# Dummy products of TensorE in the pauses for three norms: other operands and other forms

## The chip, the core and the metric

The kernel runs on one core of one Trainium2 chip. The metric is the device time of one execution in microseconds (us), as the median over several runs. A core has a matrix engine (TensorE, rows PE, with its weight loads in rows PEld), VectorE (DVE), ScalarE (ACT), GpSimd (POOL) and DMA queues issued by SyncE (SPq). Each engine runs its own list of instructions in order; they wait for one another through semaphores. TensorE multiplies a stationary operand (at most 128 rows by 128 columns, loaded by LDWEIGHTS) by a moving operand of up to 512 columns and writes to PSUM, which is `bank[:, 0..7, 512]` here. Its clock has two levels here, 1.2 and 2.4 GHz; the profile shows the granted share of the full one as PEclk.

## The reference

Two transformer blocks over 256 tokens of width 2048, all in float32. The first has three attention branches, a gated mix, a projection, and a feed-forward layer with a short convolution. The second has 16 more tokens in front (272), a full-attention layer and a layer of gated linear attention. Between the stages stand norms over each token's row:

```python
def rmsnorm(x, g):
    xf = x.astype(jnp.float32)
    y = xf * lax.rsqrt(jnp.mean(xf * xf, axis=-1, keepdims=True) + EPS)
    return (y * g.astype(jnp.float32)).astype(x.dtype)
...
x = x + rmsnorm(mix @ w_out[l], post_mix_g[l])
h = rmsnorm(x, pre_ffn_g[l])
x = x + rmsnorm(conv_ffn(h, w_up[l], conv_w[l], conv_b[l], w_down[l]), post_ffn_g[l])
...
for i in range(DEPTH_2):
    y = rmsnorm_2(h, pre_norm[i])
    ...
    h = h + rmsnorm_2(y, post_norm[i])
```

A norm of the whole row must be known before the next projection can start, so three times in the kernel the projection engine has nothing to multiply while the other engines make the norm.

## The kernel before

Weights (some 390 MB) stream from HBM in units of 128 x 1024 floats through `raw`. ACT rounds each unit to `whi` (line 602), DVE makes the rest `wlo = raw - whi` (line 1214), and TensorE forms each product in three passes of type float32r: whi by ahi, whi by alo, wlo by ahi (`PASSES`). `features` (line 1935) has the weights stationary and 256 or 272 tokens moving; `rows_of_unit` (line 2032) has the tokens stationary and 512 weight columns moving. The program text is the order: each engine's block is written out stage by stage, and no scheduler or planner stands behind it.

The stages on TensorE are, in order: projections of block one, gates, the branches' outputs (`oabc`), `wout`, **pause 1** (b = 1), `up`, `down`, **pause 2** (b = 2), the projections of the attention layer (`aqk`, `av`, `ag`), `aout`, **pause 3** (b = 3), and the stages of gated linear attention (`gqk`, `lr`, `gv`, `gg`, `gout`).

In a pause ACT squares and sums the last rows (line 693), DVE applies the gain, scales and adds to the residual (lines 1304, 1330), ACT squares the new rows (line 713), and DVE writes the normed rows `xn` (line 1393). For b = 1 the residual rows `xtok` themselves go on (line 1337). TensorE then transposes the rows by products with the identity `ident` (`turn_rows`, line 1975), ACT and DVE make `ahi` and `alo` of the result (lines 726 and 1400), and the next stage's first product waits for those (`made` in `features`).

At the head of a pause TensorE runs `keep_busy(b, n)` (line 2050): n products of two constant float32 tiles, `ones` and `ident`, 128 x 128 by 128 x 128, written to a part of PSUM that nobody reads. n is 12 in pause 1 and 36 in pauses 2 and 3. No engine waits for them; behind them on TensorE's own list stand the transposes. A float32 product stands in the trace as two records, a float32r product as one.

Of the kernel before, what the change touches and what calls it, by code (L numbers as in the profile page):

```python
# [17 lines left out]
F32 = mybir.dt.float32  # L18
# [5 lines left out]
P = 128  # L24
D = 2048
KD = D // P
TB = 256
TM = 16
T2 = TB + TM
# [98 lines left out]
def two_blocks_kernel(nc, A, out):  # L128

    ctx = ExitStack()  # L130
    with ctx:
        place_at = [(nc.sbuf_base + 31) // 32 * 32]

        def sb(name, shape, dt=F32, at_=None):

            size = int(np.prod(shape[1:])) * 4
            off = place_at[0] if at_ is None else at_
            t = nc.alloc_sbuf_tensor_at(name, shape, dt, offset=off)
            if at_ is None:
                place_at[0] = off + (size + 31) // 32 * 32  # L140
            return t
# [16 lines left out]
        ahi = sb("ahi", [P, KD * AS], F32R)  # L158
        alo = sb("alo", [P, KD * AS], F32R)
        par = sb("par", [P, N_PAR])  # L160
        ident = sb("ident", [P, P])
        ones = sb("ones", [P, P])
# [14 lines left out]
        def region(*parts, base=None):  # L177

            off, made = R2 if base is None else base, []
            for name, shape, dt in parts:  # L180
                made.append(sb(name, shape, dt, at_=off))
                off += (int(np.prod(shape[1:])) * 4 + 31) // 32 * 32
            assert off <= LIMIT, (parts[0][0], off, LIMIT)
            return made

        def ha(t, k, c0, n):

            return t[:, k * AS + c0:k * AS + c0 + n]
# [36 lines left out]
        ghi, glo, pr = region(("ghi", [P, FT, TB], F32R), ("glo", [P, FT, TB], F32R), ("pr", [P, 2, TB], F32),  # L225
                              base=R2 + 64)
        cv = sb("cv", [P, 4, TB], F32, at_=tmp_at)
        rxdiag, rxrow = msq, rstd
        FIRST_GATED = 4
        qk2, v2, v2m, gs2, cos, sin, turned2, sq2, rs2, n2, nc2, nm2, sum2, vt2, pT3, _, z2hi_first, z2lo_first = region(  # L230
            ("qk2", [P, 24, T2], F32), ("v2", [P, 2, 1024], F32), ("v2m", [P, 1024], F32R), ("gs2", [P, KD, T2], F32), ("cos", [P, T2], F32),
            ("sin", [P, T2], F32), ("turned2", [P, 2, T2], F32), ("sq2", [P, 2, T2], F32), ("rs2", [P, 2, T2], F32),
# [31 lines left out]
        bank = ctx.enter_context(nc.psum_tensor("bank", [P, 8, 512], F32))  # L264
# [136 lines left out]
        def x_updates(b, tt, c1):  # L401

            return N_XU[b] + max(n + 1 for n, (row, _, end) in enumerate(X_PIECES[b]) if row == tt and end <= c1)
# [192 lines left out]
        def _(act):  # L596
# [7 lines left out]
            def trip(ph, i, read_out, before=None, after=None, split_before=0):  # L604

                n = UNITS[ph]
                for j in range(n):
                    if before:
                        before(i, j)
                    if j >= split_before:  # L610
                        split(U0[ph] + j + LEAD, i, n)
                    chunk, _, ends = chunk_of(ph, j)
                    if ends and read_out:
                        read_out(i, chunk, U0[ph] + j, n)
                    if after:
                        after(i, j)
# [1282 lines left out]
        def _(pe):  # L1899
            PASSES = ((0, 0), (0, 1), (1, 0))  # L1900

            def unit_begin(ph, i, j):

                n = UNITS[ph]
                u = U0[ph] + j
                pe.wait_ge(wlo_ready, at(u + 1, i, n))
                chunk, begins, ends = chunk_of(ph, j)
                return u, C0[ph] + chunk, begins, ends
# [62 lines left out]
            def turn_rows(src, g):  # L1971

                for k in (2 * g, 2 * g + 1):
                    for tt in range(2):
                        mm = pe.transpose(turned(k)[:, tt * P:(tt + 1) * P], src[:, tt, k * P:(k + 1) * P], ident[:, :])  # L1975
                return mm
# [60 lines left out]
            def norm_turn(b, g):  # L2037
# [6 lines left out]
                    pe.wait_ge(act_ready, LO[f"norm{b}"] + 2 * (g - 4) + 2)  # L2044
                turn_rows(xtok if b == 1 else xnorm[b], g).then_inc(xn_turned, 1)

            def keep_busy(b, n):

                for _ in range(n):
                    pe.matmul(bank[:, 0 if b == 3 else 7, 0:P], ones[:, :], ident[:, :], start=True, stop=True)  # L2050

            def norm(b):

                keep_busy(b, 36)
                for g in range(4):
                    norm_turn(b, g)
# [83 lines left out]
            for j in range(UNITS["kvb"]):  # L2140
# [6 lines left out]
                for k in range(nk):  # L2147
                    for wp, ap in PASSES:
                        mm = pe.matmul(bank[:, 0, 0:TB], w[wp][:, k, 0:P], ha((ahi, alo)[ap], k0 + k, 0, TB),
                                       start=begins and k == 0 and (wp, ap) == (0, 0), stop=ends and k == nk - 1 and wp == 1)  # L2150
# [18 lines left out]
            for i in range(TRIPS["wout"]):  # L2169
                for j in range(UNITS["wout"]):  # L2170
                    rows_of_unit("wout", 1, i, j)
                    if (i, j) == (0, 10):
                        meta_mean(0)
            keep_busy(1, 12)
            for g in range(2):
                norm_turn(1, g)
# [174 lines left out]
            u, c, _, _ = unit_begin("lr", 0, 0)  # L2351
            bank_free("lr", c, 0, 0)
            for k in range(KD):
                cols = slice(2 * k * GL_RANK, 2 * (k + 1) * GL_RANK)
                for wp, ap in PASSES:
                    mm = pe.matmul(bank[0:2 * GL_RANK, 0, 0:T2], (whi, wlo)[wp][:, u % RING, cols], ha((ahi, alo)[ap], k, 0, T2),
                                   start=k == 0 and (wp, ap) == (0, 0), stop=k == KD - 1 and wp == 1)
# [113 lines left out]
            for i in range(TRIPS["gout"]):  # L2471
                for j in range(UNITS["gout"]):
                    u, _, begins, ends = unit_begin("gout", i, j)
                    n = 2 * i + j // 8
                    k0, nk = unit_tiles("gout", j)
                    w = [t[:, u % RING, :].rearrange("p (k n) -> p k n", k=nk) for t in (whi, wlo)]
                    for tt in range(2):
                        b = 2 * (n % 2) + tt
# [6 lines left out]
                        for k in range(nk):  # L2485
                            for wp, ap in PASSES:
                                mm = pe.matmul(bank[:, b, :], gated(ap, k0 + k)[:, tt * P:(tt + 1) * P], w[wp][:, k, :],  # L2487
                                               start=begins and k == 0 and (wp, ap) == (0, 0),
                                               stop=ends and k == nk - 1 and wp == 1)
# [86 lines left out]
```

## Time and profile before

| | us |
|---|---|
| median of 3 runs | 2333.7 |
| lowest and highest run | 2333.51, 2335.56 |
| the profiled execution, whole | 2338.52 |
| its span, first to last instruction | 2336.7 |
| TensorE busy (share of the span) | 2280.8 (98%) |
| VectorE busy | 1462.3 (63%) |
| ScalarE busy | 1187.4 (51%) |
| GpSimd busy | 253.0 (11%) |
| mean granted clock of TensorE | 0.995 |

The page gives each engine's busy time, then the span in 40 slices with the busy share in tenths. The chain of work is followed back from the last instruction, and its shares say which engine sets the end. The timeline lists instructions by their start. The cadence of a series of products, start to start, is the time that it occupies TensorE; a record's own duration is longer, because products overlap in the pipeline.

### The profile page before, as it was taken

To read this page: it belongs to the slowest core of one execution; us is meant where nothing else is said; L and a number is where in the kernel's file an instruction comes from. 1 tells how busy PE (TensorE), PEld (TensorE's weight loads), DVE (VectorE), ACT (ScalarE), POOL (GpSimd) and SP (SyncE) were. 2 spreads that over 40 slices of the span, in tenths; PEclk is the share of its full clock that TensorE was granted. 3 is DMA by queue.
4 is the path that set the end of the run, shared out by engine and by line. 5 is a ranking of instruction groups with operands and counts; after the bars stand their busy time and mean duration, and the time that the engine had idled before them with its cause. 6 is when DMAs were issued, how large, how long until landed. Compare 5 with 4: busy or idle time off the path is not lost.

```text
span 2336.7 us, 43847 instructions
## 1 busy us (share of the span) xinstructions
PE 2280.8 (98%) x17109; PEld 2145.5 (92%) x17109; DVE 1462.3 (63%) x1930; ACT 1187.4 (51%) x1769; POOL 253.0 (11%) x206
## 2 busy tenths in 40 slices
PE   7999999999999999999999999999999999999898
PEld 7898999998789999999988889999889999999886
DVE  5556644458567777777755557997665464556554
ACT  5455544445455545554544445545565454675453
POOL 0000000015002212212200001220002000001210
PEclk9999999999999999999999999999999999999999
DMA  8544466656656566566666664654335555554353
GB/s 279 176 142 145 137 206 190 194 164 187 207 157 194 182 207 190 180 205 194 194 210 194 191 187 138 188 189 143 101 109 181 172 178 169 160 154 121 115 174 141
DMA packets 258872, 405.68 MB, mean 174 GB/s; under 512 B 16655, under 2 KB 115852, under 8 KB 257708
## 3 DMA queue, kind: packets, MB, share of 16 engines
q1 hardware_dynamic: 257060, 396.87, 55.0%
q10 hardware_dynamic: 1688, 7.07, 0.9%
q8 instruction: 88, 1.44, 0.3%
q14 instruction: 36, 0.29, 0.0%
HBM read 396.32 MB, written 4.22 MB: 171 GB/s over the span
## 4 chain that ended last, share of the span: by engine, by line
PE 90%; DVE 5%; ACT 3%; issue 1%; DMA 0%; POOL 0%; ACTq 0%; DVEq 0%; SPq 0%; POOLq 0%
PE bank L1935 62%; PE bank L2032 14%; PE bank L2487 3%; PE bank L1950 2%; DVE wlo L1214 2%; ACT whi L602 1%; PE bank L2240 1%; PE bank L1975 1%; PE bank L2273 1%; PE bank L2453 1%; PE bank L2412 1%; PE bank L2214 0%; PE bank L2110 0%; PE bank L2249 0%; DVE mixtmp L1550 0%
## 5 line engine op out<-in xcount | busy, mean ns | idle before, releaser
L1214 DVE TENSOR_TENSOR wlo<-raw,whi 128x1024 fp32r<-128x1024 f32 x749 | 956.6, 1288 | 714.5 <-ACT whi L602 711.2
L1935 PE MATMUL bank<-ahi,whi 128*128 128x256 f32 (+1 forms) x4224 | 1200.4, 284 | 5.6 <-DVE lrT L1721 1.5
L1935 PE MATMUL bank<-ahi,wlo 128*128 128x256 f32 (+1 forms) x4224 | 1185.0, 281 | 0.0
L1935 PE MATMUL bank<-alo,whi 128*128 128x256 f32 (+1 forms) x4224 | 1184.9, 281 | 0.0
L602 ACT ACTIVATE whi<-raw 128x1024 fp32r<-128x1024 f32 x749 | 788.1, 1059 | 703.2 <-PE bank L1935 472.3
L1935 PEld LDWEIGHTS bank<-ahi,whi 128*128 128x128 f32 x4224 | 796.9, 189 | 15.1 <-issue 11.3
L1935 PEld LDWEIGHTS bank<-alo,whi 128*128 128x128 f32 x4224 | 797.0, 189 | 1.4 <-issue 0.2
L1935 PEld LDWEIGHTS bank<-ahi,wlo 128*128 128x128 f32 x4224 | 796.7, 189 | 0.0
L2032 PE MATMUL bank<-whi,ghi 128*128 128x512 f32 x352 | 137.2, 390 | 0.0
L2032 PE MATMUL bank<-whi,glo 128*128 128x512 f32 x352 | 137.1, 389 | 0.0
L2032 PE MATMUL bank<-wlo,ghi 128*128 128x512 f32 x352 | 137.1, 389 | 0.0
L2516 POOL CAST ghi<-pr 128x256 f32 x44 | 40.0, 908 | 469.9 <-DVE pr L1586 469.9
L1579 DVE SCALAR_TENSOR_TENSOR cv<-bank,par,cv 128x255 f32<-128x255 f32 (+1 forms) x176 | 78.8, 478 | 12.0 <-DVE cv L1579 1.5
L2032 PEld LDWEIGHTS bank<-wlo,ghi 128*128 128x128 f32 x352 | 66.1, 188 | 13.8
L2032 PEld LDWEIGHTS bank<-whi,ghi 128*128 128x128 f32 x352 | 66.1, 188 | 13.7 <-DVE wlo L1214 0.2
L2032 PEld LDWEIGHTS bank<-whi,glo 128*128 128x128 f32 x352 | 66.1, 188 | 13.7
L2498 POOL TENSOR_TENSOR glo<-pr,ghi 128x256 f32 x44 | 65.8, 1495 | 7.2 <-POOL ghi L2516 7.2
L931 ACT ACTIVATE cv<-bank,par 128x256 f32<-128x256 f32 x88 | 42.5, 563 | 38.4 <-DVE bank L1573 38.4
L1935 PE MATMUL bank<-yhi,whi 128*128 128x256 f32 x192 | 54.1, 282 | 5.0 <-DVE wlo L1214 4.8
L2508 POOL TENSOR_TENSOR mixtmp<-mixtmp 128x256 f32<-128x256 f32 x32 | 30.5, 985 | 250.3 <-DVE mixtmp L1550 250.3
L1008 ACT ACTIVATE p<-bank,nm 128x272 f32<-128x272 f32 (+1 forms) x48 | 22.9, 481 | 64.9 <-DVE nm L1632 64.9
L807 ACT ACTIVATE prob<-sbias,nmax 128x128 f32<-128x128 f32 (+1 forms) x48 | 21.5, 448 | 66.6 <-DVE nmax L1475 40.8
(335 smaller groups left out, 2340.7 us busy)
## 6 DMA issues: line engine op xcount, KB each, us to landing
raw<-in_w_up SPq DMA_DIRECT2D x176, 512.0 KB, 4.6
raw<-in_w_in SPq DMA_DIRECT2D x156, 512.0 KB, 3.8
raw<-in_attn_w_in SPq DMA_DIRECT2D x96, 512.0 KB, 4.1
raw<-in_gla_w_in SPq DMA_DIRECT2D x96, 512.0 KB, 3.8
raw<-in_w_down SPq DMA_DIRECT2D x80, 512.0 KB, 4.4
raw<-in_w_out SPq DMA_DIRECT2D x32, 512.0 KB, 4.4
raw<-in_attn_w_out SPq DMA_DIRECT2D x32, 512.0 KB, 3.7
raw<-in_gla_w_out SPq DMA_DIRECT2D x32, 512.0 KB, 4.2
```

What stands on the lines that cost most here:

```text
L602: act.activation(whi[:, u % RING, :], raw[:, u % RAW, :], ACT.Copy).then_inc(whi_ready, 1)
L931: act.activation(cv[:, t, :], bank[:, 4 * chunk + t, 0:TB], ACT.Identity, bias=par[:, bass.ds(i * 4 + (PAR["conv_b"] + r), 1)], scale=par[ ...
L1214: dve.tensor_tensor(wlo[:, u % RING, :], raw[:, u % RAW, :], whi[:, u % RING, :].bitcast(F32), ALU.subtract).then_inc(wlo_ready, 1)
L1579: dve.scalar_tensor_tensor(cv[:, t, back:TB], bank[:, 4 * chunk + t, 0:TB - back], tap, cv[:, t, back:TB], ALU.mult, ALU.add).then_inc((ta ...
L1935: mm = pe.matmul(bank[:, base + t, 0:T], w[wp][:, k, col:col + P], rhs(ap, k0 + k), start=begins and k == 0 and (wp, ap) == (0, 0), stop=e ...
L1950: mm = pe.matmul(bank[:, first_bank + tt, 0:cols[1] - cols[0]], ha((ahi, alo)[ap], k0 + k, tt * P, P), w[wp][:, k, cols[0]:cols[1]], start ...
L1975: mm = pe.transpose(turned(k)[:, tt * P:(tt + 1) * P], src[:, tt, k * P:(k + 1) * P], ident[:, :])
L2032: mm = pe.matmul(bank[:, row_bank(b, c, tt), :], tokens_of, w[wp][:, k, :], start=begins and k == 0 and (wp, ap) == (0, 0), stop=ends and ...
L2487: mm = pe.matmul(bank[:, b, :], gated(ap, k0 + k)[:, tt * P:(tt + 1) * P], w[wp][:, k, :], start=begins and k == 0 and (wp, ap) == (0, 0), ...
L2498: pool.tensor_tensor(dst, whole, high.bitcast(F32), ALU.subtract).then_inc(done, 1)
L2508: pool.tensor_tensor(mixtmp[:, 0, t, :], mixtmp[:, 0, t, :], mixtmp[:, 1, t, :], ALU.add)\
L2516: pool.tensor_copy(ghi[:, bass.ds(i * 4 + t, 1), :], pr[:, t % 2:t % 2 + 1, :]).then_inc(ffhi_ready, 1)
```

## The change

`keep_busy` no longer multiplies `ones` by `ident`. In each pause it multiplies tiles whose contents are no longer needed: `yhi` and `ylo` in pause 1, two parts of `glo` in pause 2, parts of `ahi` and `alo` in pause 3. All are float32r, with 256 moving columns (272 in pause 3). Each form is issued three times. The forms are:

- in all pauses: contiguous columns, and one column repeated over all (stride 0);
- in pauses 1 and 2 also: 16 columns out of every 32, and every second column;
- in pause 2 also: 128 of 192, 16 of 20, 2 of 4, 32 of 48 columns, and a stationary operand of every second column;
- in pauses 2 and 3 also: a stationary operand of 32 columns, operands of 64 rows, and both operands viewed as float32.

That makes 4 forms and 12 products in pause 1, 12 forms and 36 products in pause 2, 5 forms and 15 products in pause 3; the argument n is no longer used. The results go to the same unread banks. Nothing else in the program changes.

```diff
--- before.py
+++ after.py
@@ -2044,10 +2044,40 @@
                     pe.wait_ge(act_ready, LO[f"norm{b}"] + 2 * (g - 4) + 2)
                 turn_rows(xtok if b == 1 else xnorm[b], g).then_inc(xn_turned, 1)
 
+            def grid(flat, c0, n, width, pitch):
+
+                return flat[:, c0:c0 + n // width * pitch].rearrange("p (a b) -> p a b", b=pitch)[:, :, 0:width]
+
             def keep_busy(b, n):
 
-                for _ in range(n):
-                    pe.matmul(bank[:, 0 if b == 3 else 7, 0:P], ones[:, :], ident[:, :], start=True, stop=True)
+                if b == 2:
+                    moving, still = (glo[:, k:k + 8, :].rearrange("p k t -> p (k t)") for k in (12, 24))
+                    T, spare = TB, bank[:, 7, :]
+                elif b == 3:
+                    moving, still = ha(ahi, 8, 0, T2), ha(alo, 8, 16, TB)
+                    T, spare = T2, bank[:, 0, :]
+                else:
+                    moving, still = (t[:, :, :].rearrange("p k t -> p (k t)") for t in (yhi, ylo))
+                    T, spare = TB, bank[:, 7, :]
+                off = 16 if b < 3 else 0
+                L = still[:, off:off + P]
+                flat = moving[:, 0:T]
+                forms = [(L, flat, None), (L, moving[:, 0:1].to_broadcast([P, T]), None)]
+                if b < 3:
+                    forms += [(L, grid(moving, 0, T, 16, 32), 16), (L, moving[:, 0:2 * T:2], None)]
+                if b == 2:
+                    forms += [(L, grid(moving, 0, T, T // 2, 3 * T // 4), T // 2), (L, grid(moving, 0, T, 16, 20), 16),
+                              (L, grid(moving, 0, T, 2, 4), 2), (L, grid(moving, 0, T, 32, 48), 32),
+                              (still[:, off:off + 2 * P:2], flat, None)]
+                if b > 1:
+                    forms += [(still[:, off:off + 32], flat, None), (L[0:64, :], flat[0:64, :], None),
+                              (L.bitcast(F32), flat.bitcast(F32), None)]
+                for left, right, width in forms:
+                    dst = spare[0:left.shape[1], 0:T]
+                    if width is not None:
+                        dst = dst.rearrange("p (a b) -> p a b", b=width)
+                    for _ in range(3):
+                        pe.matmul(dst, left, right, start=True, stop=True)
 
             def norm(b):
 
```

TensorE's list around pause 2, before: the last products of `down` (L2032), the dummy products, the transposes of the rows `xn`, the first products of `aqk` (L1935).

```order
L2032 MATMUL bank<-whi,ghi 128x512
L2032 MATMUL bank<-whi,glo 128x512
L2032 MATMUL bank<-wlo,ghi 128x512
L2050 MATMUL bank<-ident,ones 128x128 x36
L1975 MATMUL bank<-ident,xn_112 128x128 x16
L1935 MATMUL bank<-ahi,whi 128x272
L1935 MATMUL bank<-alo,whi 128x272
```

The same place after:

```order
L2032 MATMUL bank<-whi,ghi 128x512
L2032 MATMUL bank<-whi,glo 128x512
L2032 MATMUL bank<-wlo,ghi 128x512
L2080 MATMUL bank<-glo 128x256 x27
L2080 MATMUL bank<-glo 32x256 x3
L2080 MATMUL bank<-glo 128x256 x6
L1975 MATMUL bank<-ident,xn_112 128x128 x16
L1935 MATMUL bank<-ahi,whi 128x272
L1935 MATMUL bank<-alo,whi 128x272
```

Nothing has moved; 36 products stand where 36 stood, with twice the columns and, but for three of them, in float32r. In pause 3 on TensorE, before, behind the transposes of `yT` that end `aout`:

```order
L1935 MATMUL bank<-ahi,wlo 128x272
L2317 MATMUL bank<-ident,yT 128x128 x8
L2050 MATMUL bank<-ident,ones 128x128 x36
L1975 MATMUL bank<-ident,xn_113 128x128 x16
L1935 MATMUL bank<-ahi,whi 128x256
L1935 MATMUL bank<-alo,whi 128x256
```

The same place after:

```order
L1935 MATMUL bank<-ahi,wlo 128x272
L2347 MATMUL bank<-ident,yT 128x128 x8
L2080 MATMUL bank<-ahi,alo 128x272 x6
L2080 MATMUL bank<-ahi,alo 32x272 x3
L2080 MATMUL bank<-ahi,alo 128x272 x6
L1975 MATMUL bank<-ident,xn_113 128x128 x16
L1935 MATMUL bank<-ahi,whi 128x256
L1935 MATMUL bank<-alo,whi 128x256
```

Here 15 products stand where 36 stood; the last three of them are float32.

## Rows read from the trace of the kernel before

**Rows 1.** The page: busy time and instructions, slices, chain by engine.

```profile
PE 2280.8 (98%) x17109; PEld 2145.5 (92%) x17109; DVE 1462.3 (63%) x1930; ACT 1187.4 (51%) x1769; POOL 253.0 (11%) x206
...
PE   7999999999999999999999999999999999999898
...
PE 90%; DVE 5%; ACT 3%; issue 1%; DMA 0%; POOL 0%; ACTq 0%; DVEq 0%; SPq 0%; POOLq 0%
```

**Rows 2.** Timeline of TensorE, pause 1: start, us, instruction, idle before and releaser.

```profile
667.53 2.84 PE L2050 MATMUL bank<-ident,ones 128*128 128x128 f32 x24
671.01 1.09 PE L1975 MATMUL bank<-ident,xtok 128*128 128x128 f32 x8 [0.64 <-DVE xtok L1337]
673.21 0.36 PE L1935 MATMUL bank<-ahi,whi 128*128 128x256 f32 x1 [1.11 <-DVE alo L1400]
```

**Rows 3.** Timeline, pause 2, TensorE and the DVE rows that end its wait.

```profile
1395.55 8.20 PE L2050 MATMUL bank<-ident,ones 128*128 128x128 f32 x72
...
1406.03 0.88 DVE L1393 TENSOR_SCALAR xn<-xtok,xstat 128x512 f32<-128x512 f32 x2
...
1406.58 3.56 PE L1975 MATMUL bank<-ident,xn 128*128 128x128 f32 x16 [2.82 <-DVE xn L1393]
...
1409.89 0.37 PE L1935 MATMUL bank<-ahi,whi 128*128 128x272 f32 x1
```

**Rows 4.** Timeline of TensorE, pause 3.

```profile
1871.97 8.20 PE L2050 MATMUL bank<-ident,ones 128*128 128x128 f32 x72
1882.68 1.97 PE L1975 MATMUL bank<-ident,xn 128*128 128x128 f32 x16 [2.51 <-DVE xn L1393]
1884.87 0.36 PE L1935 MATMUL bank<-ahi,whi 128*128 128x256 f32 x1 [0.23 <-DVE alo L1400]
1885.07 0.28 PE L1935 MATMUL bank<-alo,whi 128*128 128x256 f32 x1
1885.19 0.28 PE L1935 MATMUL bank<-ahi,wlo 128*128 128x256 f32 x1
```

**Rows 5.** Timeline of TensorE: float32 products of 256 columns, in the stage `gg`.

```profile
2191.53 1.89 PE L2460 MATMUL bank<-osq,ones 128*128 128x256 f32 x8
```

**Rows 6.** Timeline of TensorE in `wout`: a wait and what follows.

```profile
583.49 0.40 PE L2032 MATMUL bank<-whi,alo 128*128 128x512 f32 x1
583.72 0.39 PE L2032 MATMUL bank<-wlo,ahi 128*128 128x512 f32 x1
585.91 0.51 PE L2032 MATMUL bank<-whi,ahi 128*128 128x512 f32 x1 [1.80 <-DVE wlo L1214]
...
588.81 0.63 PE L2032 MATMUL bank<-whi,ahi 128*128 128x512 f32 x1
589.24 0.63 PE L2032 MATMUL bank<-whi,alo 128*128 128x512 f32 x1
```

**Rows 7.** Windows: from:to length, busy (instructions) of PE, PEld, DVE, ACT, POOL, PEclk, DMA.

```profile
587.20:590.50 3.30, 3.30 (x9) 2.55 (x8) 2.06 (x2) 0.35 (x2) 0.00 (x0) 0.51 0.91 319
590.60:594.00 3.40, 3.40 (x16) 2.82 (x15) 1.23 (x1) 1.46 (x2) 0.00 (x0) 0.99 0.83 299
1403.80:1406.20 2.40, 0.00 (x0) 0.00 (x0) 1.84 (x5) 1.46 (x4) 0.00 (x0) 1.00 0.00 0
1406.40:1409.70 3.30, 3.12 (x15) 3.12 (x16) 1.61 (x5) 1.94 (x5) 0.00 (x0) 0.51 0.00 0
1409.80:1413.00 3.20, 3.20 (x28) 3.20 (x27) 3.20 (x8) 2.16 (x5) 0.00 (x0) 0.99 0.02 5
1880.80:1884.20 3.40, 1.52 (x14) 1.52 (x15) 1.82 (x5) 1.39 (x6) 0.00 (x0) 1.00 0.00 0
...
2205.00:2208.40 3.40, 1.30 (x10) 0.97 (x8) 3.40 (x3) 1.11 (x2) 3.40 (x2) 1.00 0.74 257
2208.50:2215.20 6.70, 5.27 (x24) 5.27 (x25) 6.19 (x14) 0.00 (x0) 0.83 (x1) 0.51 0.24 78
2215.30:2218.00 2.70, 2.70 (x35) 2.40 (x35) 0.00 (x0) 0.53 (x2) 0.00 (x0) 0.98 0.63 200
```

**Rows 8.** Waits of TensorE: who for whom, us in total, times, longest.

```profile
PE bank L2404 <- DVE qdec L1819: 6.8, 4, 2.0
```

## The prediction

> **What bounds the kernel now.** I read the page first. TensorE is busy 98% of the span, nearly all of the 40 slices stand at 9, and 90% of the chain that ended last lies on TensorE [rows 1]. So TensorE's list sets the time, and what is lost on it stays lost, unless a later wait of TensorE for another engine absorbs it. The latest such wait of any size is for `qdec` in the last stages, 6.8 us in four pieces [rows 8]; its DVE chain is itself fed by TensorE's earlier results, so I count nothing as absorbed.
>
> Next I read the timeline at the three pauses. In each the dummy products run first, then TensorE idles, then come the transposes. In pause 1, 24 records (12 float32 products) start at 667.53 and end at 670.37. The transposes start at 671.01 after 0.64 us of idling for `xtok`, and the first product of `up` starts at 673.21 after 1.11 us for `alo` [rows 2]. In pause 2, 72 records run from 1395.55 to 1403.75, and the transposes wait 2.82 us more, for `xn` [rows 3]. In pause 3 they run from 1871.97 to 1880.17, and the wait is 2.51 us [rows 4]. What ends each pause is DVE's norm. The dummy products end ahead of it, so their own length is free in both kernels, up to that point. Their only effect is on what TensorE's clock does next.
>
> That is the third view, the windows with the granted clock. After the wait of 1.80 us that ends at 585.91, the granted clock is 0.51 (1.2 of 2.4 GHz) from 587.2 to 590.5 and then 0.99 again [rows 6, 7]. The products of 512 columns start 0.43 us apart there (588.81 to 589.24), where at full clock they start 0.23 apart (583.49 to 583.72). In pause 2 the clock is 1.00 up to 1406.2, 0.51 from 1406.4 to 1409.7, and 0.99 after [rows 7]. In pause 3 it stays at 1.00 [rows 7], though the idling was nearly as long. Longer idling is thus answered with a stretch at the half level, in the rows 3.3 us or, once, 6.7 us long (2208.5 to 2215.2, where TensorE was busy for only 5.27) [rows 7].
>
> **The change, part by part.** The price of the products first. Float32 dummies of 128 columns: 8.20 us for 72 records, (8.20 - 0.28) / 71 = 0.112 us each [rows 3]. Float32 with 256 columns: 1.89 us for 8 records [rows 5], (1.89 - 0.38) / 7 = 0.216 each, two per product, 0.43 us a product. Float32r with contiguous 256 columns: 1885.07 to 1885.19, 0.12 us a product [rows 4].
>
> No row has a strided moving operand, a repeated column or a strided stationary one. The bounds are 0.12 us, the contiguous product of the same type and size, and 0.43 us, the same columns in float32. I take 0.12, since number of columns, type and passes are those of the row.
>
> The Trainium skill bears on this: "SBUF — State Buffer" (the note on cachelines under "Door 1") says that reads run at full bandwidth as long as a 16-byte line is hit at least twice in a row. All the forms here do that, even every second column and 2 of 4. By this rule too the forms would cost 0.12; no row shows it.
>
> *Pause 1.* 12 x 0.12 = 1.4 us where 2.8 stood. TensorE is free at about 669.0 and the transposes still start at 671.01: 2.0 us of idling in place of 0.64, with the 1.11 us before `up` still to come. The nearest row is the wait of 1.80 us amid dense products, which brought the half level, beginning some 3.0 us after the idling began (584.1 to 587.2) [rows 6, 7]. In the same manner it would begin here at about 672 and last 3.3 us, to 675.3. The products of `up` start at 673.21, so 2.1 us of dense work runs at half speed and gets 1.05 us less done. Ends: 0 (the clock doesn't fall) and 1.7 (all 3.3 us on dense work). I take **+1.1**.
>
> *Pause 2.* 33 products of 0.12 and 3 of 0.43: 4.0 + 1.3 = 5.3 us in place of 8.2. The idling grows from 2.8 to 5.7 us, 1400.9 to 1406.58. But the transposes run at the half level already [rows 3, 7], and there is no lower one. The half level may begin earlier, while nothing runs, at no cost. If it also ends where it did, the cost is nothing. If it ends later it takes in dense products of `aqk`, up to 1.7. Below nothing: before has this half level already, and more idling doesn't remove it. I take **+0.4**, near the lower end, because the trace shows the clock back once the transposes had run [rows 7].
>
> *Pause 3.* 15 products: 12 x 0.12 + 3 x 0.43 = 2.8 us in place of 8.2. TensorE idles from 1874.8 to 1882.68, 7.9 us in place of 2.5. With a wait so much longer than the 2.8 us that brought the half level in pause 2, I expect it here as well. What it costs the transposes is read from the two pauses: from the first transpose to the first product behind it is 3.31 us in pause 2 (1406.58 to 1409.89) and 2.19 in pause 3 (1882.68 to 1884.87), so 1.1 us. If the half level outlives the transposes, dense products of `gqk` add up to 1.7. The row 2208.5 to 2215.2 shows that a stretch with gaps in it is prolonged. I take 1.1 + 0.5 = **+1.6**, ends 1.1 and 2.8.
>
> A rule speaks against those small ends. "TensorE: Matmul & The Clock Gate" of the Trainium skill (Part 4, on the transpose) says that work in transpose mode doesn't bring the full clock back, since it isn't counted as busy. Pauses 2 and 3 would then cost 1.7 and 2.8 here. The trace speaks against it: the window 1406.4 to 1409.7 holds transposes alone, and from 1409.8 the clock is 0.99 [rows 3, 7].
>
> Nothing else changes. The banks are the ones used before, nobody waits for the products, and the ACT and DVE chains of the norm keep their lists. The cover for the dummies is the norm, 3.5 us in pause 1 (667.53 to 671.01) and 11.0 and 10.7 us in pauses 2 and 3; 1.4, 5.3 and 2.8 fit.
>
> **Sum**: 1.1 + 0.4 + 1.6 = +3.1 us. Against the profiled execution that is 2338.5 + 3.1 = 2341.6 (span 2339.8). That execution is 4.8 us above the median of the runs shown. The difference carries over: 2333.7 + 3.1 = **2336.8 us**, +0.13%. A difference under 0.2% (4.7 us, so up to 2338.4) can't be told from none.
>
> **Rivals.**
> 1. *The half level reaches into dense work in all three pauses.* Terms 1.7, 1.7 and 2.8: +6.2, 2339.9, slower. It decides once the clock comes back only well behind the transposes. For it: the prolonged stretch at 2208.5, and idle times two to three times as long. Against it: the row at 1409.8. The transpose rule above would give this too.
> 2. *The other forms are slower than contiguous ones, about twice.* Each of the 9 such products in pause 1 takes 0.24: 2.5 us in all, nearly the old cover, 0. Of the 24 in pause 2, 2.9 us more, 8.2 in all as before, so 0. Pause 3 has only 3 such, so it still pays 1.6, less some. Sum +1.5, 2335.2. If the clock in pause 1 simply doesn't fall, the sum is +2.0, much the same. No row shows such a form.
> 3. *They are much slower, at 0.43 us.* Pause 1: 9 x 0.31 = 2.8 more, done at 671.8, 0.8 late. Pause 2: 24 x 0.31 = 7.4 more, 12.7 us where 11.0 are free, 1.7 late, but the clock stays up and saves 1.1. Pause 3 pays 1.6. Sum +3.0, by another mechanism.
> 4. *The products don't do what idling undoes*, that is, half levels come and go by chance of when they fall, and dummies matter little. Then the change is worth 0: 2333.7. For it: 2.82 us of idling brought the half level and 2.51 did not. Against it: with 5 to 8 us of idling no such luck is left.
>
> **How the numbers follow.** Forecast 0.55; rival 1 0.20; rival 2 (with the clock that holds in pause 1) 0.13; rival 3 0.05; rival 4 0.07. The three runs of before spread over 2 us, so each case carries about 1 us either way. From rival 1 nearly all (0.17) lies above 2338.4, from the forecast and rival 3 some 0.06: slower 0.23. Faster than 2329.0 no case reaches; 0.02 is left for the unknown. Same 0.75. The range runs from 2333.0, the lower side of rivals 2 and 4, to 2340.0, the middle of rival 1.
>
> **What the profile after would show.** L2080 instead of L2050, contiguous products 0.12 us apart, and at the strided ones the start times decide between the forecast and rivals 2 and 3. Idle before the transposes of 2.0, 5.7 and 7.9 us. Windows at half clock from about 672 to 675, through the transposes of pause 2 as before, and from before 1882 to about 1886. First product of `up` still at 673.2; from first transpose to first product 3.3 us in pauses 2 and 3. The forecast is wrong if the clock stays at 1.00 in pause 1 or 3, if the half level lies on dense products for 3 us or more behind pause 2 or 3, or if the transposes start later than DVE's `xn`.

## The result and the profile after

| | before | after |
|---|---|---|
| median of 10 runs each, us | 2334.45 | 2340.89 |
| lowest, highest | 2333.06, 2338.29 | 2337.56, 2342.57 |
| profiled execution, whole | 2338.52 | 2342.54 |
| its span | 2336.7 | 2340.7 |
| its mean granted clock | 0.995 | 0.992 |

The ratio is 1.0027, 95% interval 1.0019 to 1.0035. The changed kernel is 6.4 us slower by the medians. I had forecast +3.1 and a range that ended at 2340.0; the time lies 0.9 us above it. Two timed runs of the experiments below lie far off (8065.9 us in e2_long_forms, 3264.1 us in e9_fill_all) and are left out of the ratios.

Below, a difference in medians and one by the ratio are both given where they part, because the spread of the runs is as large as the effects.

TensorE around pause 1, after (timeline: start, us, instruction, idle before and releaser), to be read beside [rows 2]:

```profile
668.12 1.90 PE L2080 MATMUL bank<-yhi,ylo 128*128 128x256 f32 x12
671.61 1.10 PE L1975 MATMUL bank<-ident,xtok 128*128 128x128 f32 x8 [1.58 <-DVE xtok L1337]
673.80 0.55 PE L1935 MATMUL bank<-ahi,whi 128*128 128x256 f32 x1 [1.10 <-DVE alo L1400]
...
678.64 0.42 PE L1935 MATMUL bank<-alo,whi 128*128 128x256 f32 x1
678.85 0.42 PE L1935 MATMUL bank<-ahi,wlo 128*128 128x256 f32 x1
679.07 1.48 PE L1975 MATMUL bank<-ident,xtok 128*128 128x128 f32 x8
```

The transposes start when they did, 3.5 us after the dummies. What is new comes behind them. The products of `up` start 0.21 us apart, where they start 0.12 apart at the full clock [rows 4]. In pauses 2 and 3, beside [rows 3, 4]:

```profile
1398.86 6.42 PE L2080 MATMUL bank<-glo 128*128 128x256 f32 x39
1409.90 3.23 PE L1975 MATMUL bank<-ident,xn 128*128 128x128 f32 x16 [4.61 <-DVE xn L1393]
1412.78 0.58 PE L1935 MATMUL bank<-ahi,whi 128*128 128x272 f32 x1
...
1875.23 3.50 PE L2080 MATMUL bank<-ahi,alo 128*128 128x272 f32 x18
1886.03 3.68 PE L1975 MATMUL bank<-ident,xn 128*128 128x128 f32 x16 [7.30 <-DVE xn L1393]
1889.36 0.56 PE L1935 MATMUL bank<-ahi,whi 128*128 128x256 f32 x1
```

The windows after (from:to, length, busy of PE, PEld, DVE, ACT, POOL, then the granted clock), beside [rows 7]:

```profile
673.20:679.90 6.70, 6.09 (x28) 6.13 (x29) 4.69 (x8) 1.61 (x3) 0.00 (x0) 0.50 0.09 24
680.40:684.00 3.60, 3.60 (x33) 3.60 (x32) 2.96 (x6) 3.60 (x8) 0.00 (x0) 1.00 0.15 51
1398.90:1405.20 6.30, 6.30 (x40) 5.39 (x38) 5.87 (x10) 3.42 (x9) 0.00 (x0) 1.00 0.76 257
1410.50:1413.80 3.30, 3.30 (x17) 3.30 (x16) 2.32 (x6) 3.15 (x8) 0.00 (x0) 0.50 0.00 0
1881.50:1891.70 10.20, 5.67 (x27) 5.67 (x28) 7.94 (x18) 7.27 (x17) 0.00 (x0) 0.50 0.01 2
1891.80:1895.00 3.20, 3.20 (x30) 3.20 (x29) 1.51 (x3) 1.04 (x3) 0.00 (x0) 1.00 0.15 17
```

The half level lasts 6.8 us behind pause 1 (673.1 to 680.0), nearly all of it over dense products. In pause 3 it lasts 10.2 us, of which 5.7 lie on work, to 2.3 us into `gqk`.

I cut both traces at fixed instructions and compared the lengths of the pieces:

| piece | before | after | difference |
|---|---|---|---|
| start to first product of `wout` | 575.6 | 576.2 | +0.6 |
| last product of `wout` to first of `down` (pause 1) | 488.8 | 491.4 | +2.6 |
| last of `down` to last transpose of `yT` (pause 2) | 476.5 | 476.6 | +0.1 |
| last transpose of `yT` to stage `lr` (pause 3) | 109.4 | 111.6 | +2.2 |
| first score product to first of `gout` | 130.9 | 129.3 | -1.6 |

The first and the last row are pieces that the change doesn't touch. The trace of before has half-level stretches at 2171 and 2208.5, the one of after has only the second (2212.6). The three pauses alone give 4.9 us; the medians say 6.4.

### The profile page after: what moved, and what is told of

It reads as the page before. It is cut to its first block, busy times and chain, and to the rows that moved or that the text cites. A ratio compares the mean times of both kernels' runs of the same rounds, so it can differ in the third digit from the quotient of the medians.

```text
span 2340.7 us, 43649 instructions
## 1 busy us (share of the span) xinstructions
PE 2277.9 (97%) x17010; PEld 2140.9 (91%) x17010; DVE 1462.5 (62%) x1930; ACT 1187.8 (51%) x1769; POOL 253.0 (11%) x206
## 4 chain that ended last, share of the span: by engine, by line
PE 90%; DVE 5%; ACT 3%; issue 1%; DMA 0%; POOL 0%; ACTq 0%; DVEq 0%; SPq 0%; POOLq 0%
PE bank L1935 62%; PE bank L2032 14%; PE bank L2517 3%; PE bank L1950 2%; DVE wlo L1214 2%; ACT whi L602 1%; PE bank L2270 1%; PE bank L1975 1%; PE bank L2303 1%; PE bank L2483 1%; PE bank L2442 1%; PE bank L2244 0%; PE bank L2140 0%; PE bank L2279 0%; DVE mixtmp L1550 0%
## 5 line engine op out<-in xcount | busy, mean ns | idle before, releaser
L1935 PE MATMUL bank<-ahi,whi 128*128 128x256 f32 (+1 forms) x4224 | 1202.6, 285 | 5.4 <-DVE lrT L1721 1.5
L1935 PE MATMUL bank<-ahi,wlo 128*128 128x256 f32 (+1 forms) x4224 | 1186.8, 281 | 0.0
L1935 PE MATMUL bank<-alo,whi 128*128 128x256 f32 (+1 forms) x4224 | 1186.7, 281 | 0.0
L1935 PEld LDWEIGHTS bank<-ahi,whi 128*128 128x128 f32 x4224 | 798.2, 189 | 14.7 <-issue 10.8
L1935 PEld LDWEIGHTS bank<-alo,whi 128*128 128x128 f32 x4224 | 798.7, 189 | 1.4 <-issue 0.2
L1935 PEld LDWEIGHTS bank<-ahi,wlo 128*128 128x128 f32 x4224 | 797.7, 189 | 0.0
L2032 PE MATMUL bank<-whi,ghi 128*128 128x512 f32 x352 | 137.2, 390 | 0.0
L2032 PE MATMUL bank<-whi,glo 128*128 128x512 f32 x352 | 137.1, 390 | 0.0
L2032 PE MATMUL bank<-wlo,ghi 128*128 128x512 f32 x352 | 137.1, 389 | 0.0
L2032 PEld LDWEIGHTS bank<-whi,ghi 128*128 128x128 f32 x352 | 66.1, 188 | 14.0 <-DVE wlo L1214 0.2
L2032 PEld LDWEIGHTS bank<-wlo,ghi 128*128 128x128 f32 x352 | 66.1, 188 | 13.7
L2032 PEld LDWEIGHTS bank<-whi,glo 128*128 128x128 f32 x352 | 66.1, 188 | 13.5
L1935 PE MATMUL bank<-yhi,whi 128*128 128x256 f32 x192 | 54.2, 282 | 5.0 <-DVE wlo L1214 4.8
```

Source lines behind the costliest of these rows:

```text
L1935: mm = pe.matmul(bank[:, base + t, 0:T], w[wp][:, k, col:col + P], rhs(ap, k0 + k), start=begins and k == 0 and (wp, ap) == (0, 0), stop=e ...
L2032: mm = pe.matmul(bank[:, row_bank(b, c, tt), :], tokens_of, w[wp][:, k, :], start=begins and k == 0 and (wp, ap) == (0, 0), stop=ends and ...
```

## The experiments

**Theory D**: only the time that TensorE idles counts; the new dummies are shorter, so the clock falls to its half level more often and for longer. **Rival F**: the other forms and operands hold the clock less well than the constants, whatever their length. Each run is timed against the kernel before on the same chip.

**e1_short_const**: the old products, but fewer.

```diff
 def keep_busy(b, n):
+    n = {1: 8, 2: 28, 3: 15}[b]
     for _ in range(n):
```

> The old constant products, 8, 28 and 15 of them: the dummy work then lasts as long as in the changed kernel (1.96, 6.44 and 3.52 us against 1.90, 6.42 and 3.50), so TensorE idles as long before the transposes. Theory D (only the length of the idling counts): about 6 us slower than the kernel before, as the changed kernel was (2334.45 to 2340.89), ratio 1.0027, with the half level in pause 1 on dense products. Rival F (the other forms and operands hold the clock less well than the constants do, length aside): near the kernel before, at most 2 us slower.

Measured: 2338.49 against 2334.77, ratio 1.0017 (1.0008 to 1.0027). It is slower with the constants too, by 3.7 us in medians. The size lies between the numbers of the two theories, and its interval overlaps the changed kernel's. Its trace shows why one execution may pay less: TensorE idled as long in pause 1 as in the changed kernel, and the clock stayed up.

```profile
666.73 1.95 PE L2051 MATMUL bank<-ident,ones 128*128 128x128 f32 x16
670.21 1.09 PE L1975 MATMUL bank<-ident,xtok 128*128 128x128 f32 x8 [1.54 <-DVE xtok L1337]
```

The window over the first products of `up`, with the clock at 1.00:

```profile
672.50:676.00 3.50, 3.50 (x29) 3.38 (x30) 3.50 (x7) 0.93 (x1) 0.00 (x0) 1.00 0.00 0
```

The piece from `wout` to `down` took 488.7 us here.

**e2_long_forms**: the changed kernel with longer series.

```diff
-                    for _ in range(3):
+                    for _ in range({1: 5, 2: 4, 3: 7}[b]):
                         pe.matmul(dst, left, right, start=True, stop=True)
```

> The changed kernel with each form issued 5, 4 and 7 times in pauses 1, 2 and 3 in place of 3: the dummy work lasts 3.0, 8.4 and 7.8 us, about as in the kernel before (2.84, 8.20, 8.20). Theory D: within 1.5 us of the kernel before. Rival F: still 5 to 7 us slower.

Measured: 2336.33 against 2334.77, ratio 1.0002 (0.9993 to 1.0011). With its length back, the change costs nothing that shows. Rival F as it stood, 5 to 7 us, falls here; an effect of the forms of up to 2.6 us is not excluded.

**e3_pause1_only**, **e4_pause3_only**, **e5_pause2_only**: the old products, shortened in one pause.

```diff
 def keep_busy(b, n):
+    n = {1: 8, 2: 36, 3: 36}[b]      # e3
...
+    n = {1: 12, 2: 36, 3: 15}[b]     # e4
...
+    n = {1: 12, 2: 28, 3: 36}[b]     # e5
```

> The kernel before with 8 constant products in place of 12 in pause 1 alone; pauses 2 and 3 as before. Theory D: this carries the largest part, 2.5 to 3 us slower, since the changed kernel's trace lost 2.6 us between the end of wout and the start of down. My prediction's term was 1.1 us. Rival F: no difference.

> The kernel before with 15 constant products in place of 36 in pause 3 alone. Theory D: 2 to 3 us slower (the changed kernel's trace lost 2.3 us between the last transposes of yT and the stage lr); my prediction's term was 1.6 us. Rival F: no difference.

> The kernel before with 28 constant products in place of 36 in pause 2 alone. Theory D: 0 to 1 us slower, since the transposes of this pause run at the half level in the trace of before already; the changed kernel's trace lost 0.1 us there. Rival G (each pause costs the same once it idles longer): 2 to 3 us slower, like pause 3 alone.

Measured: pause 1 alone 2335.95 against 2334.77, 1.0005 (0.9996 to 1.0014). Pause 3 alone 2339.15 against 2334.77, 1.0015 (1.0006 to 1.0024). Pause 2 alone 2337.31 against 2336.11, 1.0008 (0.9994 to 1.0021). Only pause 3 is clear of noise by itself. In medians the three give 1.2, 4.4 and 1.2 us, in sum 6.8; by the ratios 1.2, 3.5 and 1.9, in sum 6.6. That is about what all three cost together (6.4), so the loss is made up of the pauses, but each share is known only to some 2 or 3 us. Pause 2 alone decides nothing between theory D and rival G. Pause 1 was below expectation, because it pays in some executions and not in others: the six fastest of its 11 runs (2331.89 to 2335.95) had a granted clock of 0.996 or 0.997, the five slowest (2336.53 to 2340.61) one of 0.994 or 0.995. Its trace is one of those that pay: half level over 6.8 us from 672.9, 491.3 us from `wout` to `down`, as in the changed kernel.

In the trace of e5_pause2_only the half level lasts 6.8 us (1405.2 to 1412.1) and reaches 2.3 us into `aqk`, where the changed kernel's trace showed 3.4 us. The window over it, and the one behind:

```profile
1405.30:1412.00 6.70, 5.58 (x26) 5.58 (x27) 4.62 (x13) 4.59 (x10) 0.00 (x0) 0.50 0.00 0
1412.20:1415.00 2.80, 2.80 (x25) 2.80 (x24) 1.33 (x2) 0.50 (x2) 0.00 (x0) 1.00 0.20 23
```

The piece from `down` to `yT` took 477.6 us there, 1.0 to 1.1 more than in the traces of before and after.

**e6_none**: no dummies, `n = {1: 0, 2: 0, 3: 0}[b]`. They bound what dummies can be worth against idling through.

> No dummy products at all; TensorE idles through the three pauses. Theory D: the half level in all three, at least as long as in the changed kernel, 6 to 8 us slower than before. A rival on amounts (each pause can lose only what one half-level stretch costs, 1.7 us): 3 to 5 us slower.

Measured: 2343.13 against 2336.11, ratio 1.0022 (1.0010 to 1.0034), clock of the runs 0.988 to 0.991. In medians that is +7.0, by the ratio +5.1 (2.3 to 7.9). The change's own +6.4 lies inside that, so no difference shows between the shortened dummies and none. The times don't exclude the rival on amounts (3 to 5 us), but its premise, at most 1.7 us a pause, is too low: pause 1 alone costs 2.5 us in this trace (491.3 against 488.8).

**e7_full_cover**: `n = {1: 15, 2: 47, 3: 46}[b]`.

> 15, 47 and 46 constant products in place of 12, 36 and 36: the dummy work lasts 3.6, 10.8 and 10.5 us, up to some 0.2 us before the transposes can start. Theory D: no half level in pauses 2 and 3, 1 to 3 us faster than before. If the half level at the transposes comes from something else than the idle time: no difference. If the longer dummies delay the transposes: 0.2 to 0.5 us slower per pause.

Measured: 2335.72 against 2336.11, ratio 0.9995 (0.9985 to 1.0006). No difference can be told; the 1 to 3 us of theory D didn't show and aren't excluded. The mechanism worked, in its trace of pause 2:

```profile
1395.61 10.65 PE L2051 MATMUL bank<-ident,ones 128*128 128x128 f32 x94
1406.64 1.97 PE L1975 MATMUL bank<-ident,xn 128*128 128x128 f32 x16 [0.38 <-DVE xn L1393]
1408.84 0.36 PE L1935 MATMUL bank<-ahi,whi 128*128 128x272 f32 x1 [0.23 <-DVE alo L1400]
```

The window ahead of the transposes, TensorE busy and the clock at 1.00:

```profile
1402.00:1406.50 4.50, 4.27 (x39) 4.07 (x37) 3.93 (x8) 3.08 (x8) 0.00 (x0) 1.00 0.00 0
```

The transposes take 1.97 us, at full clock, in place of 3.56. e12_before_look has the same without longer dummies, so in some executions there was nothing to win in this pause; how much is left of it in the mean is below what the runs resolve.

**e8_narrow**: dummies as long as before, each filling 32 of the array's 128 columns.

```diff
+    for _ in range({1: 23, 2: 68, 3: 68}[b]):
+        pe.matmul(bank[0:32, 0 if b == 3 else 7, 0:TB], still[:, 16:48], moving[:, 0:TB], start=True, stop=True)
```

> Dummies of float32r with a stationary operand of only 32 columns and 256 contiguous moving columns of the dead tiles, 23, 68 and 68 of them, 0.118 us each: 2.9, 8.2 and 8.2 us, as long as before. Theory D: no difference, at most 1 us. Rival F (a product that fills a quarter of the array's columns holds the clock less): the half level right behind or inside the dummy work, 4 to 8 us slower.

Measured: 2340.00 against 2336.11, ratio 1.0009 (0.9997 to 1.0021): the times don't decide it (+3.9 us in medians, +2.1 by the ratio). The trace excludes the strong form of rival F, that narrow products count as idling, since the clock stays at 1.00 through 8.1 us of them. Behind them the wait of 2.95 us brought the half level, as the 2.82 us did in before.

```profile
1395.92 8.09 PE L2056 MATMUL bank<-glo 128*32 128x256 f32 x68
1406.96 3.58 PE L1975 MATMUL bank<-ident,xn 128*128 128x128 f32 x16 [2.95 <-DVE xn L1393]
```

The window over the narrow products:

```profile
1396.00:1404.00 8.00, 8.00 (x69) 7.12 (x67) 7.57 (x12) 4.87 (x12) 0.00 (x0) 1.00 0.62 203
```

**e9_fill_all**: the long cover, and constants in other spots where TensorE waits. Two semaphore waits (`acc_free`, `o3_root`) stand ahead of them, for the banks that they write to.

```diff
+    n = {1: 15, 2: 47, 3: 46}[b]
...
     for g in range(2):
         norm_turn(1, g)
+    fill(bank[:, 7, 0:P], 4)
...
+    if (i, j) == (0, 3):
+        pe.wait_ge(acc_free, 4 * (C0["wout"] - 2) + 4)
+        fill(bank[:, 3, 0:P], 7)
     rows_of_unit("wout", 1, i, j)
...
+    n = {(2, 0): 7, (3, 0): 8, (3, 1): 6}.get((h, d))
+    if n:
+        pe.wait_ge(o3_root, h)
+        fill(bank[:, 4, d * TB:d * TB + P], n)
     pe.wait_ge(q_dec, 2 * h + d + 1)
```

> The longer cover of e7_full_cover, and constant products in the other idle spots that are followed by a half level in the traces: 4 between the transposes of pause 1 and up, 7 before the fourth unit of wout (the wait of 1.8 us at 584), and 7, 8 and 6 before the score products in the last stage (waits of 2.0, 2.0 and 1.6 us at 2168 to 2210). Theory D: hardly any half level left, 2 to 4 us faster than the kernel before, granted clock 0.998 (the end of the program still idles). If the half levels are due to something else: no difference.

Measured: 2332.11 against 2335.28, ratio 0.9985 (0.9976 to 0.9995), clock 0.997 to 0.999. This beats both kernels, by 3.2 us in medians against the kernel before, with nothing but products that nobody reads and the two waits ahead of them. (The changed kernel was not timed beside it; the comparison with it goes by e10_short_contiguous, 2341.55 on the same chip.) Its windows over the wait in `wout`, pause 1, and the score products:

```profile
583.00:587.00 4.00, 3.77 (x24) 3.24 (x23) 3.40 (x3) 3.41 (x4) 0.44 (x1) 1.00 0.67 223
670.00:674.00 4.00, 3.79 (x32) 3.49 (x31) 4.00 (x8) 1.58 (x3) 0.00 (x0) 1.00 0.00 0
...
2200.00:2210.00 10.00, 9.48 (x82) 8.96 (x81) 9.91 (x16) 2.03 (x3) 5.27 (x3) 1.00 0.36 114
```

The only stretches at the half level in its trace are one near the start (103.8) and the one behind the last product. From the first score product to `gout` took 126.8 us, in place of 130.9 before and 129.3 after. This piece varies by itself: it took 128.2 and 128.7 in two more traces of the kernel before, and 126.8 in the trace of e2_long_forms, which fills nothing there.

**e10_short_contiguous**: one form only, contiguous float32r columns of the dead tiles, as long as in the changed kernel.

```diff
+    for _ in range({1: 15, 2: 53, 3: 28}[b]):
+        pe.matmul(bank[:, 0 if b == 3 else 7, 0:TB], still[:, 16:16 + P], moving[:, 0:TB], start=True, stop=True)
```

> One form only, float32r with contiguous columns of the dead tiles, 15, 53 and 28 products: 1.9, 6.4 and 3.5 us of dummy work, as in the changed kernel and in e1_short_const. Theory D: 4 to 6 us slower than before, like those two. Rival F: if operands with data hold the clock better or worse than constants, this differs from e1_short_const by over 2 us.

Measured: 2341.55 against 2335.28, ratio 1.0028 (1.0018 to 1.0038), the changed kernel's result, with none of its odd forms. By the medians it differs from e1_short_const by 2.6 us, but the intervals overlap (1.0018 to 1.0027), so no effect of data against constants is shown, and none of 2 us is excluded. Its trace of pause 1, with dummies as long as in the changed kernel (1.88 us against 1.90) and the same wait:

```profile
667.29 1.88 PE L2056 MATMUL bank<-yhi,ylo 128*128 128x256 f32 x15
670.78 1.09 PE L1975 MATMUL bank<-ident,xtok 128*128 128x128 f32 x8 [1.61 <-DVE xtok L1337]
```

The windows over the half level and behind it:

```profile
672.60:675.80 3.20, 2.83 (x13) 2.86 (x14) 3.20 (x7) 1.38 (x3) 0.00 (x0) 0.50 0.00 0
676.00:679.00 3.00, 3.00 (x29) 3.00 (x28) 1.35 (x2) 1.17 (x4) 0.00 (x0) 1.00 0.22 44
```

Here the half level lasted 3.4 us (672.5 to 675.9), and the piece from `wout` to `down` took 489.9 us, 1.1 more than before.

**e11_before_look** and **e12_before_look**: the unchanged kernel, for two more traces.

> The kernel before once more, for its trace. Theory C (whether a wait of about 2 to 3 us brings the half level is chance, and the profiled execution my sum started from had more of them than most): the half-level stretch in pause 2 or at 2171 is missing here or in the next run, and the time is nearer 2334.5 than 2338.5. Rival: the same stretches as in the trace of before.

> As e11_before_look, a further trace of the kernel before. Theory C: at least one stretch differs between the three traces of this kernel. Rival: all the same.

Measured: 2342.17 and 2336.00. The first misses the time that theory C gave (nearer 2334.5 than 2338.5). The stretches do differ from trace to trace: the one at 2171 is missing in both. The wait of 1.8 us in `wout` brought the half level in two of the three (not in e12), the wait of 2.8 us in pause 2 in two of three (not in e12), the wait in pause 3, 2.51 us or 2.52 in each, in two of three (not in the first). e12, pause 2:

```profile
1393.96 8.20 PE L2050 MATMUL bank<-ident,ones 128*128 128x128 f32 x72
1404.99 1.97 PE L1975 MATMUL bank<-ident,xn 128*128 128x128 f32 x16 [2.83 <-DVE xn L1393]
1407.19 0.36 PE L1935 MATMUL bank<-ahi,whi 128*128 128x272 f32 x1 [0.23 <-DVE alo L1400]
```

Its window over the wait and the transposes, clock 1.00:

```profile
1401.00:1410.00 9.00, 5.94 (x50) 5.54 (x49) 7.19 (x16) 6.64 (x15) 0.00 (x0) 1.00 0.00 0
```

The same program, the same wait to 0.01 us, and another clock than in [rows 3, 7]: 1.97 us for the transposes against 3.56. In pause 3 of e12 it is the other way round, half level where [rows 7] have 1.00:

```profile
1881.20:1884.40 3.20, 3.20 (x17) 3.20 (x16) 2.89 (x7) 3.20 (x8) 0.00 (x0) 0.50 0.01 3
```

The piece from `yT` to `lr` took 111.7 us in e11 and 111.8 in e12, against 109.4 in the trace that I had started from; some half of that comes from a second stretch at the half level, at 1928 and 1922. In e12 the piece from `down` to `yT` took 475.4 us, where before and after show 476.5 and 476.6. Of the 19 timed runs of before beside these, 18 had a mean clock of 0.996 or 0.997; the execution that I had started from had 0.995. On the other two chips it was 28 of 33 and 21 of 35.

## Why the prediction was wrong

**What held.** TensorE sets the time. The dummies themselves cost nothing: in the traces of before and after, the transposes started when DVE was done, 3.5, 11.0 and 10.7 or 10.8 us after the dummies began. The sign and the mechanism held: shorter dummies, longer idling, more time at the half level. The length of the idling was near: 1.58, 4.61 and 7.30 us where I had 2.0, 5.7 and 7.9. The float32r products of every second column and of 2 in 4 took 0.23 us, most of the others 0.12 (below), so rival 2's price was right for three series, nine products, and the forecast's for the rest.

**The step that failed** is the length of the half level. I took it from rows of one execution, as if they showed the kernel: "last 3.3 us" in pause 1, "near the lower end" in pause 2 because the row's stretch ended with the transposes, and about 1 us of `gqk` in pause 3. The traces show, for each pause, how long the half level lasted:

| | dummies as before | shortened |
|---|---|---|
| pause 1 | none (5 traces) | none (e1), 3.4 us (e10), 6.8 us (after, e3) |
| pause 2 | none (e12), 3.4 us (before, e3, e4, e11) | 3.4 us (after), 6.8 us (e1, e5, e10) |
| pause 3 | none (before, e3), 3.4 us (e5, e11, e12) | 6.8 us (e1, e10), 10.2 us (after, e4) |

**Term 1, pause 1: +1.1 forecast, +2.6 in the trace.** The stretch lasted 6.8 us, from 673.1 to 680.0. It wasn't shortened by dense work in its first part, and it lay on dense work to its end. The upper end that I gave, 1.7, was built on one stretch of 3.3 us as well, though [rows 7] held one of 6.7. I used that row for pause 3 and not here. But the trace of the changed kernel is one draw too. With this wait, 1.5 to 1.6 us, the half level lasted 6.8 us in the traces of after and e3 (+2.6 and +2.5), 3.4 us in e10 (+1.1, the forecast to a tenth) and wasn't there in e1. The timed runs of e3 give +1.2 (-0.9 to +3.3), so in the mean the forecast of 1.1 may be right.

**Term 2, pause 2: +0.4 forecast, +0.1 between the two traces.** This agreement is luck, for two reasons. I took "the transposes run at the half level already" for a property of the kernel. It is one of the execution: e12 has the same wait at full clock, and the piece is 1.1 us shorter (475.4 against 476.5). Five traces have this pause as it was (before, e3, e4, e11, e12), and four of them show the half level in it. And "near the lower end" took the stretch to end as before. With the shortened dummies it lasted 6.8 us in three traces of four (e1, e5, e10: pieces of 477.6, 477.6 and 477.7), and only in the changed kernel's 3.4. So the term was too small: 1.1 us in those three against the trace of before, 2.2 or 2.3 against e12. The timed runs of e5, +1.9 by the ratio (-1.4 to +4.9), fit either.

**Term 3, pause 3: +1.6 forecast, +2.2 in the trace.** The half level outlived the transposes by more than I took (until 1891.7, 2.3 us into `gqk`, where I had about 1). It is within the bounds that I gave. Here too the base was a draw: it had no half level in this pause, e11 and e12 had, and against them the changed kernel's piece is no longer (111.6 against 111.7 and 111.8). The timed runs of e4 say +3.5 by the ratio (1.4 to 5.6), +4.4 in medians; this pause carries the largest share there, and the forecast lies at the low end of the interval.

**The sum.** The terms as the two traces show them give 2.6 + 0.1 + 2.2 = 4.9, against 6.4 by the medians. With 1.1 for pause 2, as in the three other traces, they give 5.9. The single-pause runs give 6.6 to 6.8. How the 6.4 us divide among the pauses stays open; what the traces show is that each of the three pauses can lose 1 to 3 us to a longer half level.

"The difference carries over" to the median is sound only for terms that every execution pays. The profiled execution of before lay 4.1 us above the median (2338.52 against 2334.45), the changed kernel's 1.7 above its own (2342.54 against 2340.89). So the two traces differ by less (4.0) than the medians do (6.4). The clock fits this, as an estimate: half-level time counts half in the mean clock and costs half its length where there is work, so 0.0015 of clock (0.995 against 0.996 or 0.997 in most timed runs) is 3.5 us. One stretch that only the trace of before has is seen, at 2171, worth 1.6 us; on the other side it lacks the one in pause 3. The rest stays open.

**Rivals.** Rival 1 gave 2339.9 and came nearest. Its condition, a clock that comes back only well behind the transposes, held in pauses 1 and 3 of the changed kernel's trace; in pause 2 only about 1 us of it lay on dense products, in e1, e5 and e10 2.3 to 2.5 us. Its prices were 1.7, 1.7 and 2.8 where that trace shows 2.6, 0.1 and 2.2. I had given it 0.20 and argued against it with the row at 1409.8, one case out of those that can occur. What I read there about transposes held: in pause 3 of e1 the half level ran from 1879.1 to 1885.9 over idling and transposes only, and the clock was up for the first product of `gqk` at 1886.1. Rival 4 was wrong as a forecast, but its remark was the important one: something beside the length of a wait decides, and I allowed only 1 us for chance about each case. That made the range too narrow: the ten runs of before spread over 5 us, of which the first three showed 2. My answer to rival 4 held as well: in pauses 2 and 3 all ten waits of 4.6 us and more, in six traces, brought the half level.

**The chances**: faster 0.02, same 0.75, slower 0.23. The outcome, +0.27% with an interval from 0.19% to 0.35%, is slower.

## What to carry to other kernels

Dummy products that keep TensorE's clock up must be counted in microseconds on the engine and not in instructions: with cheaper products the kernel lost 6.4 us, as much as without any, as far as the runs can tell (7.0 in medians, 2.3 to 7.9 by the ratio). Filling the shorter waits (1.6 to 2.0 us here) as well as the long ones, up to the time when the work can go on, was worth 3.2 us in all. When a cost comes and goes from one execution to the next, don't take one profiled execution as the base of a sum: compare its mean clock with that of the timed runs first, and take more than one trace of each kernel: three traces of the kernel before spanned 2334.2 to 2340.3 us.

## What the runs showed of the hardware

The dead-tile products are a small measurement of forms. In the changed kernel's trace, series of the same shape: contiguous columns first, then every second column (start, length of the series, count), then 2 columns of 4, then 64 rows:

```profile
668.12 0.52 PE L2080 MATMUL bank<-yhi,ylo 128*128 128x256 f32 x3
...
669.38 0.64 PE L2080 MATMUL bank<-yhi,ylo 128*128 128x256 f32 x2
...
1401.54 0.64 PE L2080 MATMUL bank<-glo 128*128 128x256 f32 x2
...
1403.17 0.62 PE L2080 MATMUL bank<-glo 64*128 64x256 f32 x3
```

Contiguous: (0.52 - 0.28) / 2 = 0.12 us apart. Every second column: 0.64 - 0.41 = 0.23 apart, and the same for 2 columns out of 4 (the row at 1401.54). One repeated column, 16 of 32, 16 of 20, 32 of 48 and 128 of 192 columns, a stationary operand of every second column, and one of 32 columns came at 0.11 to 0.12; only right behind a slow series was the first interval longer (0.14 to 0.15). Operands of 64 rows stand (0.62 - 0.28) / 2 = 0.17 apart in the mean of two intervals, the second of them 0.12; in the longer series of e2_long_forms (pause 3) all from the second on are 0.12 to 0.13. So the switch to the form costs time there, and the form itself doesn't. The note on cachelines in "SBUF — State Buffer" of the Trainium skill (under "Door 1"), which the prediction named beside its 0.12, says that two hits in a 16-byte line suffice for full bandwidth. For these two forms the trace doesn't agree: each has two elements in a line, and a product takes 0.23 us where the contiguous one takes 0.12. The same note says that each access that crosses to a new line pays a penalty, without its size; these forms cross twice as often per column as the contiguous one, and the prediction left that half out.

Whether a wait brings the half level wasn't decided by its length alone. A wait of 1.80 us at 584 did in two of three traces of the same kernel. In e2_long_forms a wait of 3.51 us in pause 3 did not:

```profile
1869.66 7.29 PE L2080 MATMUL bank<-ahi,alo 128*128 128x272 f32 x42
1880.46 1.97 PE L1975 MATMUL bank<-ident,xn 128*128 128x128 f32 x16 [3.51 <-DVE xn L1393]
```

The windows over the wait and over what follows, both at 1.00:

```profile
1876.90:1880.40 3.50, 0.06 (x1) 0.00 (x0) 2.92 (x7) 2.24 (x6) 0.00 (x0) 1.00 0.00 0
1880.50:1884.00 3.50, 3.27 (x27) 3.06 (x28) 2.27 (x6) 2.85 (x8) 0.00 (x0) 1.00 0.00 0
```

A second cause of spread has nothing to do with the change. In the traces of e6_none, e8_narrow and e11_before_look, and in none of the others, TensorE waits for `wlo` in `aout`; the wait ends between 1784.8 and 1788.2 us, and a half-level stretch follows:

```profile
PE bank L1935 <- DVE wlo L1214: 2.1, 1, 2.1
```

The piece from `down` to `yT` is about 4 us longer there (480.3 in e11 and 480.5 in e8, against 476.5 in before, which has the same half level in pause 2). What decides it was not tried, and stays open. It means that some runs of any of these kernels carry about 4 us more, which no comparison of single runs should explain.
